# Rotary halves exchanged by vector and scalar copies in place of permutation products

## What is computed

```
def rope(t, pos):
    half = HEAD_DIM // 2
    ...
    t1, t2 = tf[..., :half], tf[..., half:]
    out = jnp.concatenate([t1 * cos - t2 * sin, t2 * cos + t1 * sin], axis=-1)

q = rope((h @ w_q + b_q).reshape(bsz, s, N_Q_HEADS, HEAD_DIM), pos)
k = rope(k.reshape(bsz, s, N_KV_HEADS, HEAD_DIM), pos)
```

## Time and profile before

| | |
|---|---|
| median of 3 runs | 1178.98 us (1178.84 to 1180.38) |
| the profiled execution | 1179.31 us, span 1177.5 us |
| mean granted TensorE clock | 0.984 |
| TensorE busy | 1096.9 us, 93% of the span |
| VectorE busy | 321.3 us, 27% |
| ScalarE busy | 197.2 us, 17% |
| Pool busy | 39.4 us, 3% |
| chain that ended last | TensorE 67%, DMA 30%, VectorE 2%, ScalarE 1% |

### The profile page before, as it was taken

The page is one execution under the profiler, slowest core; times in us unless marked ns, Lnnn a source line. Parts: engine busy times, 40 slices in busy tenths (PEclk is TensorE's granted clock), DMA queues, the critical chain, the costliest instruction groups (busy, mean ns, idle before and its releaser), DMA issues.

```text
span 1177.5 us, 25173 instructions
## 1 busy us (share of the span) xinstructions
PE 1096.9 (93%) x11769; PEld 629.0 (53%) x11769; DVE 321.3 (27%) x435; ACT 197.2 (17%) x280; POOL 39.4 (3%) x35
## 2 busy tenths in 40 slices
PE   7999999999999999999989969899997789999776
PEld 6888888889763354354446315344632344354233
DVE  4554454459660030031021002202200220022013
ACT  5444434446630000000000000000000000000002
POOL 3000000002100000000000000000000000000000
PEclk9999999999999999999999999999999899999988
DMA  9985655533479999999999999999999999999993
GB/s 346 387 290 182 206 184 180 189 150 126 149 281 390 423 381 424 428 421 426 425 428 420 426 427 421 427 425 427 422 425 427 424 424 425 426 421 425 428 423 140
DMA packets 58129, 417.87 MB, mean 355 GB/s; under 512 B 5682, under 2 KB 11876, under 8 KB 33444
## 3 DMA queue, kind: packets, MB, share of 16 engines
q1 hardware_dynamic: 56080, 410.94, 85.7%
q0 software_dynamic: 1440, 4.46, 1.0%
q10 hardware_dynamic: 500, 0.80, 0.2%
HBM read 414.09 MB, written 2.10 MB: 353 GB/s over the span
## 4 chain that ended last, share of the span: by engine, by line
PE 67%; DMA 30%; DVE 2%; ACT 1%; issue 0%; SPq 0%; ACTq 0%; DVEq 0%
DMA weights<-in_moe_w 29%; PE psum L844 25%; PE psum L877 13%; PE psum L747 8%; PE psum L749 8%; PE psum L748 8%; DVE hid_t L1668 1%; DMA raw<-in_pool_w 1%; PE psum L959 1%; DVE sil L1666 1%; PE psum L813 1%; PE psum L823 0%; PE psum L755 0%; PE psum L1080 0%; PE psum L859 0%
## 5 line engine op out<-in xcount | busy, mean ns | idle before, releaser
L844 PE MATMUL psum<-weights,xg 128*32 128x512 f32 (+1 forms) x5072 | 494.9, 550 | 47.1 <-DMA weights<-in_moe_w 47.1
L844 PEld LDWEIGHTS psum<-weights,xg 128*32 128x32 f32 x5072 | 181.8, 112 | 357.7 <-issue 321.4
L877 PE MATMUL psum<-weights,hid_t 128*32 128x256 f32 x4480 | 247.3, 380 | 12.9 <-DVE hid_t L1668 8.4
L877 PEld LDWEIGHTS psum<-weights,hid_t 128*32 128x32 f32 x4480 | 151.6, 110 | 105.2 <-issue 13.7
L1666 DVE TENSOR_TENSOR sil<-sil,psum 128x1536 f32<-128x1536 f32 (+3 forms) x16 | 21.1, 1321 | 494.8 <-PE psum L844 494.1
L1529 DVE TENSOR_TENSOR low<-raw,high 128x2048 fp32r<-128x2048 f32 x50 | 114.6, 2291 | 85.6 <-ACT high L1243 85.4
L1243 ACT ACTIVATE high<-raw 128x2048 fp32r<-128x2048 f32 x51 | 97.8, 1918 | 84.4 <-PE psum L749 81.2
L747 PE MATMUL psum<-high,a_hi 128*128 128x512 f32 x224 | 87.3, 390 | 0.9 <-DVE a_lo L1566 0.9
L749 PE MATMUL psum<-low,a_hi 128*128 128x512 f32 x224 | 87.2, 389 | 0.0
L748 PE MATMUL psum<-high,a_lo 128*128 128x512 f32 x224 | 87.2, 389 | 0.0
L1299 ACT ACTIVATE y_hi<-psum 128x768 fp32r<-128x768 f32 (+1 forms) x7 | 5.0, 719 | 489.7 <-PE psum L877 489.7
(11 more groups left out here) (242 smaller groups left out, 628.3 us busy)
## 6 DMA issues: line engine op xcount, KB each, us to landing
weights<-in_moe_w SPq DMA_DIRECT2D x128, 1792.0 KB, 35.2
weights<-in_moe_w SPq DMA_DIRECT2D x48, 2048.0 KB, 38.5
raw<-in_ffn_w SPq DMA_DIRECT2D x42, 1024.0 KB, 8.1
weights<-in_moe_w SPq DMA_DIRECT2D x16, 1024.0 KB, 37.2
raw<-in_w_q SPq DMA_DIRECT2D x4, 1024.0 KB, 5.1
raw<-in_w_o SPq DMA_DIRECT2D x4, 1024.0 KB, 4.9
x_res<-in_x SPq DMA_DIRECT2D x2, 512.0 KB, 5.7
raw<-in_pool_w SPq DMA_DIRECT2D x1, 1024.0 KB, 10.0
```

Source lines behind the costliest of these rows:

```text
L844: mm = pe.matmul(UP[c][g * BLK:(g + 1) * BLK, r, :], xg[:, k_, r * BLK:(r + 1) * BLK], w[:, g], start=k_ == 0, stop=k_ == DT - 1)
L877: mm = pe.matmul(Y[g * BLK:(g + 1) * BLK, r, :], hid_t[c][:, r, at_:at_ + BLK], w[:, b, g * GW:(g + 1) * GW], start=i == 0 and b == 0 and ...
```

## The change

Both permutations by TensorE are gone. A copy of 32 partitions by VectorE or ScalarE writes to another group of 32 partitions.

- Keys: VectorE waits for `kv_done`, adds the bias from the key bank in four instructions of 64 partitions, which also put each head on both halves of the partitions, and exchanges the halves by four 32-partition copies. This stands where split(U_Q) stood.
- Queries: ScalarE, after the bias addition of unit m, waits for `biased` and `roped` and exchanges two groups by two copies into `rope_z`; VectorE exchanges the other two at the head of rotate(m). The sine product then reads `rope_z` in SBUF instead of a PSUM bank.
- The low part of U_Q is done by Pool, before the bias additions of L700; `queries(0, 0)` waits for it and for `a_lo_ready`.
- Order: on TensorE queries(0,0) comes before turn_values, and spread_keys and the four permute are gone. On ScalarE add_bias for the keys is gone, split(U_Q+2) comes before the loading of the Exp table, and add_bias of unit 0 before split(U_Q+3).

```diff
@@ Pool
             pool.wait_ge(xn_ready, 2 * NT + 1)
+            pool.wait_ge(split_hi, U_Q - U_DENSE + 1)
+            pool.tensor_tensor(low[slot(U_Q)][:], raw[slot(U_Q)][:], high[hslot(U_Q)][:].bitcast(F32),
+                               ALU.subtract).then_inc(pool_low, 1)
             pool.wait_ge(bo_in, 16)
...
-                pool.wait_ge(biased, m + 2)
+                pool.wait_ge(biased, m + 1)
                 pool.wait_ge(roped, m + 1)
@@ TensorE
-            def spread_keys():
...
-            def permute(m):
...
                 if n == 0:
-                    pe.wait_ge(split_lo, u - U_DENSE)
+                    if m == 0:
+                        pe.wait_ge(a_lo_ready, 2 * DT)
+                        pe.wait_ge(pool_low, 2)
+                    else:
+                        pe.wait_ge(split_lo, u - U_DENSE - 1)
                     if m >= 2:
-                        pe.wait_ge(biased, m)
+                        pe.wait_ge(biased, m - 1)
...
-            spread_keys()
+            queries(0, 0)
             turn_values()
-            queries(0, 0)
             queries(0, 1)
@@ ScalarE
+                mm.then_inc(biased, 1)
+                act.wait_ge(biased, m + 1)
+                act.wait_ge(roped, m + 1)
+                act.activation(rope_z[32:64], x[0:32], ACT.Copy)
+                act.activation(rope_z[0:32], x[32:64], ACT.Copy).then_inc(swapped, 1)
...
             split(U_Q + 1)
+            split(U_Q + 2)
             warm(ACT.Exp)
-            split(U_Q + 2)
+            add_bias(0)
+            split(U_Q + 3)
             add_bias(1)
-            split(U_Q + 3)
-            add_bias(2)
             split(U_O)
@@ VectorE
-            split(U_Q)
+
+            def swap(blocks, x):
+
+                for j in blocks:
+                    mm = dve.tensor_copy(rope_z[32 * (j ^ 1):32 * (j ^ 1) + 32], x[32 * j:32 * j + 32])
+                step(mm)
+
+            dve.wait_ge(kv_done, 1)
+            for g in range(2):
+                head = slice(g * HD, (g + 1) * HD)
+                for r in range(2):
+                    mm = dve.tensor_scalar(rope_y[r * HD:(r + 1) * HD, g, :], banks[K_OUT][head, 0:SEQ],
+                                           gains[head, 5 * DT:5 * DT + 1], None, ALU.add)
+            step(mm)
+            swap(range(4), rope_y)
             split(U_Q + 1)
...
             def rotate(m):
 
-                dve.wait_ge(permuted, m + 2)
-                step(dve.tensor_tensor(rope_z[:], bank3(Q_TURNED), both(sin), ALU.mult))
+                dve.wait_ge(biased, m + 1)
+                swap((2, 3), rope_x[:, (m + 1) % 2])
+                dve.wait_ge(swapped, m + 1)
+                step(dve.tensor_tensor(rope_z[:], rope_z[:], both(sin), ALU.mult))
                 dve.wait_ge(cosined, m + 1)
```

More of the change, by code:

```diff
@@ L381, in trunk_program @@
         PROJ = ((0, 1), (2, 3))
-        Q_OUT, Q_TURNED, V_TURNED, K_OUT, V_OUT, K_BOTH = (0, 1), 2, 3, 4, 5, (6, 7)
+        Q_OUT, V_TURNED, K_OUT, V_OUT = (0, 1), 3, 4, 5
         SCORES, ATTENDED = (5, 6), 7
@@ L400, in trunk_program @@
         moe_landed = [sem(f"moe_landed{r}") for r in range(NL)]
-        first_low = sem("first_low")
+        pool_low = sem("pool_low")
         split_hi, split_lo = sem("split_hi"), sem("split_lo")
@@ L431, in trunk_program @@
         kv_turned = sem("kv_turned")
-        biased, permuted, cosined, roped = sem("biased"), sem("permuted"), sem("cosined"), sem("roped")
+        biased, swapped, cosined, roped = sem("biased"), sem("swapped"), sem("cosined"), sem("roped")
         scored, max_ready, exped = sem("scored"), sem("max_ready"), sem("exped")
@@ L597, in pair_stat @@
             return t_[:, 4 * h:4 * h + 4]
-        ROPE = [(1, K_OUT, 5 * DT)] + [(2, Q_OUT[m % 2], 4 * DT + 2 * m) for m in range(4)]
+        N_ROPED = 5
         ROUTER_GAIN = 5 * DT + 2
@@ L695, in _ @@
             pool.tensor_tensor(low[slot(U_DENSE)][:], raw[slot(U_DENSE)][:], high[hslot(U_DENSE)][:].bitcast(F32),
-                               ALU.subtract).then_inc(first_low, 1)
+                               ALU.subtract).then_inc(pool_low, 1)
             pool.wait_ge(xn_ready, 2 * NT + 1)
+            pool.wait_ge(split_hi, U_Q - U_DENSE + 1)
+            pool.tensor_tensor(low[slot(U_Q)][:], raw[slot(U_Q)][:], high[hslot(U_Q)][:].bitcast(F32),
+                               ALU.subtract).then_inc(pool_low, 1)
             pool.wait_ge(bo_in, 16)
@@ L710, in _ @@
             pool.dma_start(row_bc[:], bc(norm_ffn[1])).then_inc(gn_in, 16)
-            pool.wait_ge(roped, len(ROPE))
+            pool.wait_ge(roped, N_ROPED)
             pool.dma_start(consts[:, C_TOK:C_TOK + SEQ + N_SLOT], slots).then_inc(slots_in, 16)
@@ L774, in dense_feed_forward @@
                     else:
-                        pe.wait_ge(first_low, 1)
+                        pe.wait_ge(pool_low, 1)
                     if half == 0 and kind == "w1":
@@ L992, in _ @@
             mm.then_inc(unit_used, 1)
-            perm = consts[:, C_PERM:C_PERM + P]
-            def spread_keys():
[L999 to L1007, removed]
             def turn_values():
@@ L1090, in project @@
                     if t == 0:
-                        pe.wait_ge(biased, len(ROPE))
+                        pe.wait_ge(biased, 4)
                     else:
-                        pe.wait_ge(roped, len(ROPE))
+                        pe.wait_ge(roped, N_ROPED)
                         pe.wait_ge(probs_out, 4)
@@ L1107, in project @@
                     mm.then_inc(unit_used, 1)
-            spread_keys()
+            queries(0, 0)
             turn_values()
-            queries(0, 0)
             queries(0, 1)
             queries(1, 0)
-            permute(0)
             queries(1, 1)
@@ L1117, in _ @@
             queries(2, 0)
-            permute(1)
             queries(2, 1)
@@ L1122, in _ @@
             queries(3, 0)
-            permute(2)
             turn_probs(0, 1)
@@ L1129, in _ @@
             scores(2)
-            permute(3)
             attend(1)
@@ L1370, in _, with add_bias @@
                                scale=gains[:, 3 * DT + d:3 * DT + d + 1]).then_inc(a_hi_ready, 1)
[L1371 to L1381, removed]
+            def add_bias(m):
+                act.wait_ge(unit_used, U_Q + m + 1)
+                if m:
+                    act.wait_ge(roped, m)
+                x = rope_x[:, (m + 1) % 2]
+                for k in range(2):
+                    col = 4 * DT + 2 * m + k
+                    mm = act.activation(x[:, k, :], banks[Q_OUT[m % 2]][:, k * SEQ:(k + 1) * SEQ], ACT.Identity,
+                                        bias=gains[:, col:col + 1])
                 mm.then_inc(biased, 1)
+                act.wait_ge(biased, m + 1)
+                act.wait_ge(roped, m + 1)
+                act.activation(rope_z[32:64], x[0:32], ACT.Copy)
+                act.activation(rope_z[0:32], x[32:64], ACT.Copy).then_inc(swapped, 1)
             def exponentials(m, h):
@@ L1414, in take_attended @@
                                ACT.Copy).then_inc(ot_hi_ready, 1)
-            add_bias(0)
             act.wait_ge(unit_used, U_KV + 1)
@@ L1428, in _ @@
             exponentials(0, 1)
-            add_bias(3)
+            add_bias(2)
             take_probs(0, 0)
@@ L1434, in _ @@
             exponentials(1, 1)
-            add_bias(4)
+            add_bias(3)
             take_attended(0)
@@ L1753, in both @@
                 return table.unsqueeze(1).to_broadcast([P, 2, SEQ])
-            def bank3(b):
-                return banks[b].rearrange("p (a t) -> p a t", a=2)
             def by_chunk(t_):
@@ L1772, in rotate_keys @@
             def rotate_keys():
-                dve.wait_ge(permuted, 1)
-                dve.tensor_tensor(rope_y[:], bank3(K_BOTH[0]), both(cos), ALU.mult)
-                step(dve.tensor_tensor(rope_z[:], bank3(K_BOTH[1]), both(sin), ALU.mult))
+                dve.tensor_tensor(rope_y[:], rope_y[:], both(cos), ALU.mult)
+                step(dve.tensor_tensor(rope_z[:], rope_z[:], both(sin), ALU.mult))
                 dve.tensor_tensor(k_t[:], rope_y[:], rope_z[:], ALU.add).then_inc(roped, 1)
```

## The result

The changed kernel takes 1182.35 us (median of 12 runs, 1180.63 to 1183.63), the kernel before 1179.36 us beside it (12 runs, 1178.41 to 1181.05). The ratio is 1.0022, 95% interval 1.0014 to 1.0030: slower by 2.6 us by the ratio (the two medians differ by 3.0). The interval, 0.14 to 0.30%, is clear of zero but lies on both sides of the 0.2% that the forecast set as its bar for a change. The forecast was +0.45. On the 1178.98 us of the forecast, 1.0022 is 1181.6 us.

What follows compares the result with a forecast made beforehand. Attention was taken as a tie of TensorE and VectorE: turn_probs(0,0) 0.9 us later, then 0.9 more against 0.8 of slack, gave +0.45 on the 1178.98 us median, 1179.4 us; range 1176.9 to 1182.2.

Steps and rivals of the forecast that it cites:

- The likeliest case: The forecast itself: attention 0.45 us longer, 1179.4 us in all, no change that can be measured; chance 0.40.
- copies at 0.69 us: Upper bound for a 32-partition copy in attention: 0.27 us more for each of ten that count, +3.15 us in all.
- The tie of VectorE and TensorE: In attention both engines set the pace, so the 5.5 us of work leaving TensorE turn largely into waits for VectorE.
- Copies at 0.42, no overlap: VectorE's 32-partition copies within SBUF were to take 0.42 us each, run end to end.
- Rival B: Copies run at one column a cycle, or Pool holds them up: +3.15 to +4.2 us, 1182.1 to 1183.2 us; chance 0.12.
- turn_probs(0,0) 0.9 us later: VectorE's longer list in attention was to start this TensorE step at 295.15 us, 0.9 us later than before.
- The circle behind it: After turn_probs(0,0), VectorE gets 0.9 us more for rotate(2) against 0.8 of slack, moving scores(2) from 305.08 to 305.55.
- Pool at zero: Pool's added subtraction before the bias additions was counted as costing nothing, with 2.7 us to spare beyond its 4.56.
- A: TensorE's clock falls to half in its new 2.6 us wait in attention: +1.2 us, 1180.6 us; chance 0.24.
- C: VectorE keeps up in attention because copies and bias additions overlap or are shorter: 1176.8 us; chance 0.16.
- D: A shift of attention is absorbed in the expert stage behind it: 1179.0 us; chance 0.08.
- The last permutation is not won: Its 1.05 us on TensorE brings nothing, since scores(3) waits for ScalarE's exponentials(2,1), which follow scores(2).

Runs made afterwards that it cites:

- e9: The changed kernel with Pool's cosine products cut to 2 columns and 6, 12 and 1 identity products filling TensorE's waits; 1179.12 us, ratio 1.0000.
- e8: The changed kernel with keys spread and queries permuted by TensorE again, leaving Pool's low part of U_Q and the new order; 1179.32 us, ratio 1.0004.
- e1: The changed kernel with Pool's four cosine products cut to 2 of 512 columns; 1180.33 us, ratio 1.0008.
- e7: The changed kernel with 8, 10 and 5 identity products filling TensorE's waits; 1181.62 us, ratio 1.0025.
- e5: The changed kernel with each of Pool's cosine products split into four instructions of 128 columns; 1181.27 us, ratio 1.0016.
- e6: The changed kernel with only keys exchanged by copies, queries permuted by TensorE, and Pool's cosine products in four pieces; 1178.40 us, ratio 0.9996.
- e10: The changed kernel with all four copies of a query unit on ScalarE and none on VectorE; 1182.46 us, ratio 1.0030.
- e3: The changed kernel with only the keys exchanged by copies and the queries permuted by TensorE as before; 1178.59 us, ratio 0.9994.
- e11: The changed kernel with all four copies of a query unit on VectorE and none on ScalarE; 1185.45 us, ratio 1.0058.

## Why the prediction was right, and where it was wrong

The time on its own basis, 1181.6 us, lies in the range but at its upper end, and the sign is a slowdown that can be measured, to which 0.22 was given. The likeliest case did not happen, and that the range holds the result is luck: its upper end was set by copies at 0.69 us, and the copies took 0.42. The slowdown came from a cost that the sum had put at zero.

- **The tie of VectorE and TensorE, and 5.5 us that turn into waits**: right. VectorE has no wait for another engine from 272.3 to 300.0 us. scores(0) starts 0.80 us earlier in the stage than before, forecast 1.0; TensorE waits 2.01 before it, forecast 1.5. The second wait, before turn_probs(0,0), was to be 2.6 us, with over 2 as a sign of being right, and is 0.94: the clock at half for 3.4 us makes TensorE's work 1.7 us longer, and 0.94 + 1.7 is the forecast wait.
- **Copies at 0.42, no overlap; four bias additions at 0.478**: right (0.42 to 0.43; 1.97 for the four, forecast 1.91). ScalarE's copies take 0.63, forecast 0.61. That they end before VectorE needs them is right too, but they also push ScalarE's next split back by their own 1.27 us, which the sum had not (0.38 below). Rival B in the shape "one column a cycle" is out.
- **turn_probs(0,0) 0.9 us later**: right, 0.94 (296.70 - 264.21 = 32.49 against 294.24 - 262.69 = 31.55). But two errors cancel in it: the split beside Pool is 0.68 longer and the first key copy 0.45, and the sink step is 1.07 shorter.
- **The circle behind it costs 0.9 less the 0.8 of slack, scores(2) +0.47**: this is the step that failed. scores(2) starts 2.17 us later in the stage (308.70 - 264.21 = 44.49 against 305.01 - 262.69 = 42.32). From weigh(0,0)'s start (+0.99) to weigh(1,1)'s end (+3.31) VectorE gains delays of 0.88 (weighing step beside Pool), 0.38 (a high part that ScalarE gives late), 0.89 (the exchange) and 1.07 (the four-column addition beside Pool), and gives back 0.85, the hole that it had ahead of maxima_of(1): 0.99 + 0.88 + 0.38 + 0.89 + 1.07 - 0.85 = 3.36. Less the 0.7 of slack that was there (TensorE started 0.77 us behind VectorE before, 0.07 after), and 0.44 for turn_probs(1,0), which TensorE now does while it waits, this is scores(2)'s start (3.31 - 0.70 - 0.44 = 2.17); its slower clock adds 0.62, and its end is 2.79 late. All that follows carries this on. Take Pool's products out and hold the clock (e9), and nothing is left of the step: scores(2) starts 0.03 us later than before, and the stage is +0.04, forecast 0.45.
- **Pool at zero**: right for the subtraction by itself (e8, +0.02), but it moves Pool's bias additions onto the first key copy (0.45 us, given as a bound only), and wrong for the cosine products that stay. I asked what Pool does to VectorE only in the exchange of the keys. The products are released by ScalarE's bias additions and by `roped`, and both move against VectorE's list when VectorE gets longer; before, three of them stood beside PSUM reads. The row that said so was in hand, 1.24 us for eight columns, and I used it inside a sum of 6.46 us without asking why it was so long. The Trainium skill ("Advanced Engine Details and Errata", section "VectorE Performance Modes") says that VectorE's second SBUF port is shared with GpSimd, and that GpSimd instructions and VectorE instructions in a 2-port mode block each other. The traces show the blocking for a two-input product of four columns too (1.23 us instead of 0.16), and for the length of a whole instruction.
- **A, the clock falls in the new wait**: happened, behind the 2.01 us before scores(0) (and again near 308 us), and not where A had it, before turn_probs(0,0). Its price by itself is 1.02 us (e1 against e9, where the fall is before turn_probs(0,0)), forecast 1.2. Beside Pool's stalls it is worth 0.19 (e7 against after).
- **C**: out, both waits are there. **D**: out, the last part is 841.5 against 841.6; the shift is carried one for one, as said.
- **The last permutation is not won, scores(3) waits for ScalarE**: seen in e9 (1.04 us) and e5 (1.05). In after, attend(1) at the slower clock fills that wait, but the limit stands: scores(3) starts 0.14 us behind ScalarE's last exponential (315.45), as before (311.14), and those follow scores(2). So it is 2.79 later, as the end of scores(2) is.

## What to carry to other kernels

Before moving work onto or ahead of an engine that shares SBUF with another, lay the two timelines over each other: every operation of Pool that will now meet a VectorE operation with all its inputs in SBUF can cost up to Pool's own length, however short the VectorE operation is. An operation that is far longer than its column count asks for in the profile of before is a warning that such a meeting exists already. And work taken off an engine that ties with another is no gain; here only the part that did not lengthen the other's list inside the loop (the keys) kept any of it, 0.9 us of the stage and too little for the runs to show.

## What the runs showed of the hardware

- VectorE and Pool shut each other out for whole instructions when VectorE's inputs are all in SBUF: four columns of VectorE took 1.23 us instead of 0.16, two columns of Pool 2.24 us instead of 0.20. Single-input operations are hit as well: a copy of 32 x 512 took 0.87 us instead of 0.42. An operation with an input in PSUM is not: before, a maximum beside Pool took 0.96 us as elsewhere, and the subtraction of L1820, with one input in PSUM and one in SBUF, 0.69.
- Four Pool products of 128 columns take 1.70 us alone (e6) and 2.03 beside short VectorE operations (e5), where one of 512 takes 1.27 to 1.30, and 3.75 to 3.76 us beside a split. They shorten the longest of VectorE's stalls, not Pool's.
- Copies of 32 partitions to another group of 32, 512 columns in SBUF: 0.42 to 0.43 us on VectorE, end to end, 0.63 on ScalarE.
- The clock went to half behind single waits of 1.73 us (e10), 2.01 us (after) and 2.42 us (e1), and not behind waits of 0.55 us (e3), 1.04 us (e9), 1.33 us (e1) or 1.65 us (e11). Behind waits of 0.37 and 1.36 us with four transposes between them (after, at 306 and 308 us) it did. At half the clock, 16 score products take 1.73 us instead of 1.11 and the 16 of attend(1) 2.17 us.
